# A projection's products in another order, splits woven into slabs, and a product with a scaled identity in place of scale and transpose

## The chip, the core and the metric

The kernel runs on one core of one Trainium2 chip, as one program. Its time is the device time of one execution in microseconds (us). The engines of the core run their own instruction streams side by side and wait for each other by semaphores: PE (TensorE) multiplies and transposes, DVE (VectorE), ACT (ScalarE) and POOL (GpSimd) work on tiles, and SP only issues DMAs here. PE reads its operands from SBUF and writes into the eight banks of PSUM. A PE transpose is one matmul instruction with the identity.

## The reference, cut to what matters

A first network (two layers of a hybrid mixer with a feed-forward part) makes `x`, 256 tokens of 1024 numbers. A second network of two layers follows, and the change is in that one alone. Of its layer:

```python
def modulate(x, shift, scale): return x * (1 + scale) + shift
for l in range(2):
    # context tokens (256): layer 0 whole, layer 1 only their k and v; latent tokens (256): whole
    h  = modulate(rms_norm_2(x, norm1_g[l]), sh1, sc1)
    p  = h @ w_in[l]                      # 1024 -> 2560: a (512), q (512), k (512), v (512), c (512)
    q, k = qk_heads(q, q_norm_g, rope), qk_heads(k, k_norm_g, rope)
    o  = diff_attn(q, k_all, v_all, lam)
    x += g1 * (concat[chunk_gmlp(a), rms_norm_2(o, subln_g), conformer_conv(c)] @ w_out)
    h2 = modulate(rms_norm_2(x, norm2_g[l]), sh2, sc2)
    x += g2 * ((silu(dwconv(h2 @ w_gate)) * (h2 @ w_val)) @ w_down)
def rms_norm_2(x, g): return x * rsqrt(mean(x * x) + EPS) * g
```

`conformer_conv` is a depthwise convolution of 31 taps over `a * sigmoid(g)` of the two halves of c, a layer norm and a silu. All is float32.

## The kernel before

Every product is made of high and low halves. A weight arrives in slabs of 256 rows by 512 columns (`SLAB_K` = 2 blocks of 128 rows). ACT rounds a slab into `whi`, DVE takes the rest into `wlo`, and the activations are kept the same way (`act2_h`, `act2_l`; the profile prints `act_h`, `act_l`). Each 128x128 block of an activation meets a slab's row block in three matmuls: high by high, high by low, low by high. Rows are tokens in tiles of 128: T = 4 tiles in layer 0 (latent and context), 2 in layer 1, except k and v and the first normalization there, which have 4. A slab of a 4-tile product is 24 matmuls of 512 columns, of a 2-tile product 12.

`Planner` (`plan_second`) lists `Step`s in one order. Each engine walks that same list and issues its own part of each step, so the list fixes the order on every engine. `weave(slabs, others)` puts a step `(at, st)` ahead of slab number `at`. At a slab's step ACT rounds and DVE splits the slab three ahead (`AHEAD`), which needs the buffer of the slab that PE used four before.

The steps that matter:

- `norm2`: POOL makes the root of each row (`rstd4`, L951, L926, L927), DVE multiplies `x` by it into `p` (L1387), one instruction a tile. `modsplit` k (eight, one for each 128 columns): PE turns that block of all tiles into one of banks 4 to 7 (L1776), DVE applies gain and shift (L1395), ACT makes the high half (L1100), DVE the low half (L1403, one step late). The first slab of the next product needs k = 0 and 1.
- the projection in five products of four slabs: c, q, k, a, v. Beside them: `cglu`, `cT` (PE turns c, ACT copies it to `cin`), `c_taps` in eight parts (DVE does the 31 taps of one half of the channels, L1525 and L1527; ACT weighs and POOL adds those of the other, L1160, L967, L974), `qk_sums` and `qk_scale` (DVE, L1420 to L1456; roots on POOL), `qkT2` (PE turns normalized q and k through banks 4 to 7, twice each; ACT copies the even ones out, DVE the odd ones, L1462), `gelu`, `ln`, `ln_scale` (L1542 to L1555).
- `agate` (PE, the product with `w_s`), which waits for `ln_scale` and stands first in the attention's list; then attention with units `att2_s`, `_v`, `_t`, `_e`, `_m`, and `subln` on its output.
- `ysplit` (eight: PE turns the merged branches, L1776, ACT and DVE L1408 make the halves), and `residual` with `w_out_2`.
- `norm2` again and the feed-forward part: per 512 columns `w_gate_2` and `w_val_2`, four PSUM banks each, in a turn over seven banks (`pl.turns = tuple(range(7))`); then `w_down_2` on banks 0 to 3.

## Time and profile before

| | |
|---|---|
| Median of three runs | 2446.95 us (2436.7 to 2447.53) |
| Profiled execution | 2444.05 us, its span 2442.4 us |
| PE busy in the span | 2222.0 us, 91% |
| DVE, ACT, POOL busy | 58%, 44%, 12% |
| The second network | from about 1356 us on |
| Idle PE ahead of transposes of `p`, whole span | 73.0 us |

The page shows busy times by engine and the costliest groups of instructions. What one place costs is read in the stretches of time, where each instruction has its start, its length and, in brackets, the idle time ahead of it with what ended it. A busy PE means that matmuls overlap: their starts, not their lengths, show the pace.

### The profile page before, as it was taken

The page shows a single profiled execution, that of the slowest core. Times are in us where ns is not written, and L with a number is a line of the kernel's source. Part 1 is how long each engine was busy: PE and PEld are TensorE (multiplying, and loading weights), DVE is VectorE, ACT ScalarE, POOL GpSimd, SP SyncE. Part 2 cuts the span into 40 slices and gives each one's busy share as a digit, 9 for nine tenths or more (in the row PEclk, how much of TensorE's full clock was granted, in tenths as well). Part 3 has the DMA queues.
Part 4 walks back from the last instruction along what each step waited for, and adds up shares of the span by engine and source line. Part 5 has one row for each costly group of instructions (what it writes and reads, how often), then busy time and mean ns, then how long its engine had stood idle before and what let it go on. Part 6 is the DMA issues. An engine that isn't in the chain of part 4 may idle for free. (4 is left out here: it accounts for less than half of the span.)

```text
span 2442.4 us, 31205 instructions
## 1 busy us (share of the span) xinstructions
PE 2222.0 (91%) x11948; PEld 1803.7 (74%) x11948; DVE 1421.3 (58%) x2234; ACT 1063.3 (44%) x1753; POOL 304.7 (12%) x310
## 2 busy tenths in 40 slices
PE   8998999899999989899999797789999998778999
PEld 6776677778777766777787675567888886658987
DVE  4655485554456555755454598755555337866664
ACT  4444555444344434554444454523232225454342
POOL 0007121100000062221000073100000001500000
PEclk9998999999999989999999898789999999889999
DMA  7553334466556534345656321222333334234654
GB/s 234 185 179 133 117 129 142 157 214 203 199 188 210 167 118 142 97 144 175 236 170 192 130 69 52 70 69 70 104 129 97 124 99 147 69 105 131 202 174 149
DMA packets 171842, 349.28 MB, mean 143 GB/s; under 512 B 11824, under 2 KB 23216, under 8 KB 171696
## 3 DMA queue, kind: packets, MB, share of 16 engines
q1 hardware_dynamic: 171696, 347.29, 43.7%
q8 instruction: 97, 1.59, 0.3%
q14 instruction: 49, 0.40, 0.1%
HBM read 346.19 MB, written 1.05 MB: 142 GB/s over the span
## 5 line engine op out<-in xcount | busy, mean ns | idle before, releaser
L820 DVE TENSOR_TENSOR wlo<-wraw,whi 128x1024 fp32r<-128x1024 f32 (+1 forms) x538 | 646.0, 1214 | 712.9 <-ACT whi L1017 710.9
L1017 ACT ACTIVATE whi<-wraw 128x1024 fp32r<-128x1024 f32 (+1 forms) x552 | 557.7, 1026 | 603.7 <-PE psum L1773 280.0
L1773 PE MATMUL psum<-whi,act_h 128*128 128x512 f32 (+2 forms) x1424 | 578.7, 406 | 30.4 <-DVE wlo L820 21.8
L1773 PE MATMUL psum<-wlo,act_h 128*128 128x512 f32 (+2 forms) x1424 | 557.4, 391 | 0.0
L1773 PE MATMUL psum<-whi,act_l 128*128 128x512 f32 (+2 forms) x1424 | 557.1, 391 | 0.0
L1773 PEld LDWEIGHTS psum<-whi,act_h 128*128 128x128 f32 x1424 | 275.6, 194 | 100.2 <-DVE wlo L820 25.6
L1773 PEld LDWEIGHTS psum<-whi,act_l 128*128 128x128 f32 x1424 | 274.4, 193 | 57.7
L1773 PEld LDWEIGHTS psum<-wlo,act_h 128*128 128x128 f32 x1424 | 275.4, 193 | 48.7
L1773 PE MATMUL psum<-act_h,whi 128*128 128x512 f32 (+1 forms) x704 | 243.8, 346 | 14.8 <-DVE cacc L1395 6.3
L1773 PE MATMUL psum<-act_l,whi 128*128 128x512 f32 (+1 forms) x704 | 239.6, 340 | 0.0
L1773 PE MATMUL psum<-act_h,wlo 128*128 128x512 f32 (+1 forms) x704 | 239.1, 340 | 0.0
L1773 PE MATMUL psum<-whi,hid_h 128*128 128x512 f32 x440 | 173.9, 395 | 0.8 <-DVE ft L1357 0.8
L1773 PE MATMUL psum<-wlo,hid_h 128*128 128x512 f32 x440 | 172.6, 392 | 0.0
L1773 PE MATMUL psum<-whi,hid_l 128*128 128x512 f32 x440 | 172.3, 392 | 0.0
L1773 PEld LDWEIGHTS psum<-act_h,whi 128*128 128x128 f32 x704 | 136.2, 193 | 32.9 <-issue 9.3
L1773 PEld LDWEIGHTS psum<-act_h,wlo 128*128 128x128 f32 x704 | 136.1, 193 | 14.4
L1773 PEld LDWEIGHTS psum<-act_l,whi 128*128 128x128 f32 x704 | 136.3, 194 | 13.2
L1776 PE MATMUL psum<-ident,p 128*128 128x128 f32 x228 | 44.4, 372 | 73.0 <-DVE p L1387 32.7
L1773 PEld LDWEIGHTS psum<-whi,hid_h 128*128 128x128 f32 x440 | 83.4, 190 | 19.2 <-DVE ft L1357 1.2
L1776 PEld LDWEIGHTS psum<-ident,p 128*128 128x128 f32 x228 | 40.0, 200 | 77.8 <-DVE p L1387 34.4
L1773 PEld LDWEIGHTS psum<-whi,hid_l 128*128 128x128 f32 x440 | 83.4, 190 | 17.7
L1773 PEld LDWEIGHTS psum<-wlo,hid_h 128*128 128x128 f32 x440 | 83.4, 189 | 17.1
(268 smaller groups left out, 2772.8 us busy)
## 6 DMA issues: line engine op xcount, KB each, us to landing
wraw<-in_w_in SPq DMA_DIRECT2D x136, 512.0 KB, 4.4
wraw<-in_w_gate SPq DMA_DIRECT2D x104, 512.0 KB, 4.2
wraw<-in_w_mod_pieces SPq DMA_DIRECT2D x96, 512.0 KB, 4.7
wraw<-in_w_ffn_in SPq DMA_DIRECT2D x80, 512.0 KB, 4.4
wraw<-in_w_ffn_out SPq DMA_DIRECT2D x44, 512.0 KB, 4.1
wraw<-in_w_down SPq DMA_DIRECT2D x44, 512.0 KB, 4.3
wraw<-in_w_val SPq DMA_DIRECT2D x40, 512.0 KB, 4.2
wraw<-in_w_branch SPq DMA_DIRECT2D x32, 512.0 KB, 4.8
```

The lines of the kernel that those rows point to most:

```text
L820: eng.tensor_tensor(wlo[:, i, 0:st.n, 0:st.w], wraw[:, st.s % RING_W, 0:st.n, 0:st.w], whi[:, i, 0:st.n, 0:st.w].bitcast(F32), ALU.subtrac ...
L1017: nc.scalar.activation(whi[:, d % RING_S, 0:st.n, 0:st.w], wraw[:, s % RING_W, 0:st.n, 0:st.w], ACT.Copy).then_inc(sem("slab_rounded"), 1)
L1773: return nc.tensor.matmul(out, lhsT, rhs, start=start, stop=stop)
L1776: return nc.tensor.transpose(out, src, ident[:, :])
```

## The change

Five things are altered, all in the second network.

1. `norm2`: DVE writes `diag`, the identity times the root of each row, 128x128 a tile, instead of `x` times the root. `modsplit` on PE multiplies `x` (stationary) with `diag` (moving) instead of transposing `p`; both are float32.
2. The eight `modsplit` steps stand no longer ahead of the product: four ahead of its first slab, two ahead of the second, two ahead of the third. The `ysplit` steps are woven into `w_out_2` likewise, whose slabs now go by row blocks 0, 6, 2, 4 (`order`).
3. The projection goes q, k, c, a, v. `qk_sums` and `qk_scale` come from slab 4 and slab 9 on, `cglu` at 13, `cT` at 14, the eight parts of the taps at 14 to 19, `qkT2` at 16 instead of 18, `gelu` at 18, `ln` at 19.
4. In attention, `subln` and its parts come behind the other steps of their round, not in the middle.
5. The turn of banks starts at bank 0 in the feed-forward part (`pl.gemm_banks = 0`).

```diff
+def gemm(..., order=None, **more):
+    order = order or range(0, nk, SLAB_K)
-        for k in range(0, nk, SLAB_K):
+        for at, k in enumerate(order):
...
+        def between(ss):
+            return [(0, st) for st in ss[:4]] + [(1, st) for st in ss[4:6]] + [(2, st) for st in ss[6:]]
...
-        gc = project(C_C, T, ready)
-        gq = project(C_Q, T)
+        gq = project(C_Q, T, ready)
         gk = project(C_K, 4)
+        gc = project(C_C, T)
...
-        for i, (g, tiles, at) in enumerate(((gq, T, 8), (gk, 4, 13))):
+        for i, (g, tiles, at) in enumerate(((gq, T, 4), (gk, 4, 9))):
...
-        others = [(5, cglu), (6, ct)] + [(at, st) for at, st in zip((7, 7, 11, 12, 12, 17, 17, 18), parts)]
-        others += qk + [(17, gelu), (18, qkt), (18, aln[0]), (19, aln[1])]
+        others = ss + [(13, cglu), (14, ct)] + [(at, st) for at, st in zip((14, 15, 15, 16, 17, 17, 18, 19), parts)]
+        others += qk + [(18, gelu), (16, qkt), (19, aln[0]), (20, aln[1])]
-        pl.steps += weave(gc + gq + gk + ga + gv, others)
+        pl.steps += weave(gq + gk + gc + ga + gv, others)
...
-                    att += pending[:1]
+                    behind += pending[:1]
...
+            att += behind
...
-        residual("w_out_2", "act2", KD, 0, {st.k: drained(st.bank) for st in ss}, True)
+        residual("w_out_2", "act2", KD, 0, {st.k: drained(st.bank) for st in ss}, True, between(ss), order[::SLAB_K])
-        pl.turns = tuple(range(7))
+        pl.turns, pl.gemm_banks = tuple(range(7)), 0
...
-                        dve.tensor_scalar(p[:, t, 0:D], x[:, t, :], rstd4[:, t:t + 1], None, ALU.mult
+                        dve.tensor_scalar(diag[:, t, :], ident[:, :], rstd4[:, t:t + 1], None, ALU.mult
...
-                        ins = turn(psum[:, st.bank[0], t * P:(t + 1) * P], p[:, t, a:a + P])
+                        ins = dot(psum[:, st.bank[0], t * P:(t + 1) * P], x[:, t, st.k * P:(st.k + 1) * P], diag[:, t, :])
```

On DVE in layer 0 of the second network, before, the copies of turned q and k (L1462) stand behind the last taps, and the layer norm follows:

```order
L1436 TENSOR_TENSOR p<-p,ssq 128x512
L1439 TENSOR_TENSOR p<-p,rows 128x512
L1527 SCALAR_TENSOR_TENSOR cacc<-cin,cols,cacc 128x2x243
L1527 SCALAR_TENSOR_TENSOR cacc<-cin,cols,cacc 128x2x242
L1527 SCALAR_TENSOR_TENSOR cacc<-cin,cols,cacc 128x2x241
L1462 COPY qT<-psum 128x512 x2
L1462 COPY kT<-psum 128x512 x2
L1542 TENSOR_REDUCE lnm<-p 128x4
```

At the same place on DVE of the changed kernel (its line numbers are 5 higher here), the copies are L1467 and the taps L1530 and L1532:

```order
L1532 SCALAR_TENSOR_TENSOR cacc<-cin,cols,cacc 128x2x253
L1532 SCALAR_TENSOR_TENSOR cacc<-cin,cols,cacc 128x2x254
L1532 SCALAR_TENSOR_TENSOR cacc<-cin,cols,cacc 128x2x255
L1467 COPY qT<-psum 128x512 x2
L1467 COPY kT<-psum 128x512 x2
L825 TENSOR_TENSOR wlo<-wraw,whi 128x1024
L1532 SCALAR_TENSOR_TENSOR cacc<-cin,cols,cacc 128x2x255
L1532 SCALAR_TENSOR_TENSOR cacc<-cin,cols,cacc 128x2x254
```

The copies moved ahead of the last 15 taps, but they stand behind the first 16, all of which now come behind the last `qk_scale`.

PE turns q and k in that step; with the semaphores that it waits for, in the changed kernel (the row of three more that follows each of these is left out):

```order
L1781 MATMUL psum<-ident,p 128x128 [waits psum_free5,qk_normed]
...
L1781 MATMUL psum<-ident,p 128x128 [waits psum_free6]
...
L1781 MATMUL psum<-ident,p 128x128 [waits psum_free7]
...
L1781 MATMUL psum<-ident,p 128x128 [waits psum_free4]
...
L1781 MATMUL psum<-ident,p 128x128 [waits psum_free5]
...
L1781 MATMUL psum<-ident,p 128x128 [waits psum_free6]
...
L1778 MATMUL psum<-whi,act_h 128x512 [waits psum_free0,slab_split]
```

The fifth and sixth of the eight groups take banks 5 and 6 again, which ACT's and DVE's first copies free; four slabs of v stand behind this step (two before).

On PE at the start of layer 0's feed-forward part, before, the last transposes and the first matmuls of `w_gate_2` are:

```order
L1776 MATMUL psum<-ident,p 128x128 [waits psum_free7,xn_out]
L1776 MATMUL psum<-ident,p 128x128 x3
L1776 MATMUL psum<-ident,p 128x128 [waits psum_free4,xn_out]
L1776 MATMUL psum<-ident,p 128x128 x3
L1773 MATMUL psum<-act_h,whi 128x512 [waits slab_split,psum_free4,mod_lo]
```

In the changed kernel the first slab's matmuls wait for other banks, and the products with `diag` stand between slabs:

```order
L1778 MATMUL psum<-act_h,whi 128x512 [waits slab_split,psum_free0,mod_lo]
...
L1778 MATMUL psum<-act_h,whi 128x512 [waits psum_free3]
...
L1778 MATMUL psum<-act_h,wlo 128x512
L1778 MATMUL psum<-diag,x 128x128 [waits psum_free5,xn_out]
L1778 MATMUL psum<-diag,x 128x128 x3
L1778 MATMUL psum<-diag,x 128x128 [waits psum_free6,xn_out]
L1778 MATMUL psum<-diag,x 128x128 x3
```

The first slab takes banks 0 to 3 instead of 4, 5, 6 and 0, and half of the turning moved behind it.

## Rows read from the trace of the kernel before

**Rows 1.** The costliest groups: transposes of `p`, busy and mean, idle before and releasers
```profile
L1776 PE MATMUL psum<-ident,p 128*128 128x128 f32 x228 | 44.4, 372 | 73.0 <-DVE p L1387 32.7
```

**Rows 2.** Stretches: length; busy (count) of PE, PEld, DVE, ACT, POOL; PEclk; DMA
```profile
1475.00:1491.00 16.00, 0.00 (x0) 0.00 (x0) 15.58 (x15) 4.72 (x5) 9.04 (x6) 0.56 0.22 66
...
1653.00:2000.00 347.00, 346.68 (x1633) 284.13 (x1634) 161.83 (x195) 98.04 (x128) 0.00 (x0) 0.99 0.33 105
```

**Rows 3.** In order of time (start, length), layer 0: normalization, slab pace, a small operation
```profile
1356.09 2.74 DVE L1387 TENSOR_SCALAR p<-x,rstd 128x1024 f32<-128x1024 f32 x4 [3.72 <-POOL rstd L927]
...
1358.89 5.96 PE L1776 MATMUL psum<-ident,p 128*128 128x128 f32 x28 [11.44 <-DVE p L1387]
...
1363.67 0.68 DVE L1403 TENSOR_TENSOR act_l<-cacc,act_h 128x512 fp32r<-128x512 f32 x1
...
1366.01 0.47 PE L1773 MATMUL psum<-whi,act_h 128*128 128x512 f32 x1
...
1378.37 1.23 DVE L820 TENSOR_TENSOR wlo<-wraw,whi 128x1024 fp32r<-128x1024 f32 x1 [1.88 <-ACT whi L1017]
1383.81 1.23 DVE L820 TENSOR_TENSOR wlo<-wraw,whi 128x1024 fp32r<-128x1024 f32 x1 [4.21 <-ACT whi L1017]
...
1523.30 0.35 DVE L1483 TENSOR_SCALAR p<-psum,ri 128x128 f32<-128x128 f32 x1
```

**Rows 4.** In order of time, layer 0: taps, turning of q and k, `ln`, gate
```profile
1403.93 9.92 DVE L1527 SCALAR_TENSOR_TENSOR cacc<-cin,cols,cacc 128x482 f32<-128x482 f32 x7
...
1433.88 13.82 POOL L974 TENSOR_TENSOR cacc<-cacc,ctmp 128x504 f32<-128x504 f32 x8 [2.33 <-ACT ctmp L1160]
...
1446.51 7.32 DVE L1527 SCALAR_TENSOR_TENSOR cacc<-cin,cols,cacc 128x504 f32<-128x504 f32 x8
...
1474.10 2.25 DVE L820 TENSOR_TENSOR wlo<-wraw,whi 128x1024 fp32r<-128x1024 f32 x1
1491.06 5.20 PE L1776 MATMUL psum<-ident,p 128*128 128x128 f32 x32 [16.47 <-DVE p L1439]
1493.07 0.69 DVE L1462 COPY qT<-psum 128x512 f32<-128x512 f32 x1
...
1496.90 1.21 DVE L1542 TENSOR_REDUCE lnm<-p 128x4 f32<-128x1024 f32 x1
...
1504.52 1.22 DVE L1555 TENSOR_TENSOR p<-p,rows 128x1024 f32<-128x1024 f32 x1
1507.01 1.89 PE L1773 MATMUL psum<-p,wsT 128*128 128x256 f32 x8
```

**Rows 5.** PE in order of time: transposes; float32 products at full and half clock
```profile
1398.79 1.03 PE L1776 MATMUL psum<-ident,p 128*128 128x128 f32 x8
...
1534.26 1.13 PE L1773 MATMUL psum<-p,aT 128*128 128x128 f32 x8
...
2175.89 2.08 PE L1773 MATMUL psum<-p,aT 128*128 128x128 f32 x8
```

**Rows 6.** PE in order of time, layer 0: merged branches, and start of the feed-forward part
```profile
1583.67 3.65 PE L1776 MATMUL psum<-ident,p 128*128 128x128 f32 x16 [3.34 <-DVE act_l L1408]
...
1639.67 5.62 PE L1776 MATMUL psum<-ident,p 128*128 128x128 f32 x28 [7.62 <-DVE p L1387]
...
1653.33 0.77 PE L1773 MATMUL psum<-act_h,whi 128*128 128x512 f32 x1 [6.30 <-DVE cacc L1395]
```

**Rows 7.** Layer 1: normalization, taps, turning of q and k, gate, start of `w_down_2`
```profile
2033.01 4.70 PE L1776 MATMUL psum<-ident,p 128*128 128x128 f32 x24 [7.63 <-DVE p L1387]
...
2061.82 5.32 DVE L1527 SCALAR_TENSOR_TENSOR cacc<-cin,cols,cacc 128x241 f32<-128x241 f32 x7
...
2120.96 5.09 PE L1776 MATMUL psum<-ident,p 128*128 128x128 f32 x24 [11.58 <-DVE p L1439]
...
2137.66 0.71 PE L1773 MATMUL psum<-p,wsT 128*128 128x128 f32 x4 [0.24 <-ACT p L1063]
...
2377.62 0.51 PE L1773 MATMUL psum<-whi,hid_h 128*128 128x512 f32 x1 [0.77 <-DVE ft L1357]
```

More of the change, by code:

```diff
@@ L161, in weave, with gemm @@
     return out + slabs[i:]
-def gemm(pl, weight, layer, act, tiles, nk, col0, width, evac, row0=0, kt0=0, ready=(), turned=False, **more):
+def gemm(pl, weight, layer, act, tiles, nk, col0, width, evac, row0=0, kt0=0, ready=(), turned=False, order=None, **more):
     steps = []
+    order = order or range(0, nk, SLAB_K)
     hasdict = isinstance(ready, dict)
@@ L171, in gemm @@
             banks.append(pl.gemm_bank())
-        for k in range(0, nk, SLAB_K):
+        for at, k in enumerate(order):
             n = min(SLAB_K, nk - k)
-            last = k + n == nk
+            last = at == len(order) - 1
             st = Step(kind="slab", s=len(pl.slabs), weight=weight, layer=layer, row=row0 + k, n=n, col=col0 + a, w=w,
-                      act=act, kt=kt0 + k, tiles=tiles, banks=banks, first=k == 0, last=last, c=c, a=a, evac=evac,
+                      act=act, kt=kt0 + k, tiles=tiles, banks=banks, first=at == 0, last=last, c=c, a=a, evac=evac,
                       turned=turned, **more)
@@ L197, in gemm @@
             elif (pl.mod_queue or pl.mod_last) and tiles == 2 and st.s >= 3 * RING_W:
-                at, slabs_in = k // SLAB_K, -(-nk // SLAB_K)
-                if pl.mod_queue and at % 4 == 0 and at + 3 < slabs_in:
+                if pl.mod_queue and at % 4 == 0 and at + 3 < len(order):
                     st.after = mod_ride(pl, pl.next_bank())
@@ L439, in norm @@
                        halves=[("mod_half", pl.tick("mod_half"))] if tiles == 4 else []) for k in range(KD)]
-            pl.steps += ss
-            return {st.k: [("mod_lo", st.lo)] for st in ss}
-        ready = norm(0, 4, l > 0)
+            return {st.k: [("mod_lo", st.lo)] for st in ss}, between(ss)
+        def between(ss):
+            return [(0, st) for st in ss[:4]] + [(1, st) for st in ss[4:6]] + [(2, st) for st in ss[6:]]
+        ready, ss = norm(0, 4, l > 0)
         pl.first_slab[l] = len(pl.slabs)
@@ L760, in build @@
         rstd4 = sb("rstd4", [P, 4], F32, two)
+        diag = sb("diag", [P, 4, P], F32, two)
         kT = sb("kT", [P, B_HEADS, 4 * P], F32, two)
@@ L1843, in _ @@
                     ins.then_inc(full(bk), 1)
-                if st.kind in ("modsplit", "ysplit"):
+                if st.kind == "modsplit":
                     need(pe, st.waits)
                     fill(pe, st.bank)
-                    a = st.k * P if st.kind == "modsplit" else st.col
                     for t in range(st.tiles):
-                        ins = turn(psum[:, st.bank[0], t * P:(t + 1) * P], p[:, t, a:a + P])
+                        ins = dot(psum[:, st.bank[0], t * P:(t + 1) * P], x[:, t, st.k * P:(st.k + 1) * P], diag[:, t, :])
+                    ins.then_inc(full(st.bank), 1)
+                if st.kind == "ysplit":
+                    need(pe, st.waits)
+                    fill(pe, st.bank)
+                    for t in range(st.tiles):
+                        ins = turn(psum[:, st.bank[0], t * P:(t + 1) * P], p[:, t, st.col:st.col + P])
                     ins.then_inc(full(st.bank), 1)
```

18 lines of the change are left out of this document (9 added, 9 removed).

## The prediction

> **What bounds the kernel now.** I read the busy shares and costliest groups first. PE is the bound, but its transposes of `p` have 73.0 us of idle time ahead of them [rows 1]: PE stands there waiting for somebody's vector work. The stretches say where. In the feed-forward part of layer 0 PE is busy 346.68 of 347 us, while from 1475 to 1491 us it is busy for nothing and DVE for 15.58 [rows 2]. The order of time then gives four kinds of hole: the scaling of `x` ahead of a normalization's first transpose [rows 3, 6, 7], the wait for the last `qk_scale`, 16.47 us in layer 0 and 11.58 in layer 1 [rows 4, 7], 3.34 us ahead of the last merged branches, and 6.30 us ahead of the first matmul of `w_gate_2` in layer 0 [rows 6]. The change aims at each. The question at each is what is late next. Below, S is the start of PE's first transpose after a normalization before the change, S' the same place after it.
>
> **Prices.** A slab of 24 matmuls takes PE 5.44 us (two DVE splits that each follow a freed slab, 1378.37 and 1383.81) [rows 3], of 12 matmuls 2.72. A transpose takes 0.11 us at full clock (8 in 1.03, the last one's tail of some 0.2 taken off) [rows 5] and 0.21 at half clock (28 in 5.96) [rows 3]. The product with `diag` isn't in the trace. Its nearest row is the float32 product `psum<-p,aT`, also of 128 by 128. It has two records for each instruction: four instructions a unit give x8. That is 0.125 us a record at full clock and 0.24 at half [rows 5], so 0.25 and 0.48 us an instruction. The bounds are one record (the transposes' price) and the 0.48. I take two records.
>
> The Trainium skill (TensorE: Matmul & The Clock Gate, "Terms") says that transpose mode is 4 times faster for FP32. The trace shows a factor of 2.3 at full clock. By the page's factor the woven products of a 4-tile stage would take 7 us, not 4, and the sum would be some 9 us worse.
>
> **Normalization.** DVE writes 128 columns a tile instead of 1024. Four of the old take 2.74 us; a 128-column operation with a scalar takes 0.35 at most [rows 3], and overlapped somewhat less. I take 0.15 us each between ends of 0.1 and 0.35. S' is therefore S - 2.1 us with four tiles (ends 2.3 and 1.3) and S - 1.0 with two.
>
> Then, layer 0, first normalization. Before, the first slab starts at S + 7.1 (1366.01 - 1358.89), and `act_l` of k = 1 was ready at S + 5.5 (1363.67 + 0.68) [rows 3]. After, 16 instructions stand ahead: 32 records, the first 20 at half clock, 6.3 us; with DVE's first block 1 us later, the first slab starts at about S' + 6.8. The other 16 instructions cost 2 us behind each of two slabs. Four slabs end at S' + 6.8 + 21.8 + 4 = S' + 32.6 = S + 30.5, against S + 28.9: 1.6 us later. The woven splits of the slabs (each 1.23 us [rows 3] in DVE's chain and a rounding that it waits for, some 2.2 us) stay behind PE here. In layer 1 the q slabs have only 2.72 us and DVE's chain is the bound: k = 7 is ready at about S' + 21, the four slabs end at S' + 23.7.
>
> **Projection, layer 0.** `cT` now follows slab 13. It ends at S' + 32.6 + 10 x 5.44 + 1 = S' + 88, and the taps start at S' + 89.5. All 31 stand behind this point, and so do DVE's three last slab splits and four copies, and POOL's 31. Taps beside POOL's go at 1.42 us (7 in 9.92), alone at 0.92 (8 in 7.32), a split beside POOL at 2.25 [rows 4]. POOL pairs with DVE there; I take 1.48 a tap for it, between 1.42 and the 1.73 of another stretch (8 in 13.82) [rows 4], so some 46 us, to S' + 135.5. In its time DVE does three splits (6.7), four copies (1 us each between 0.69 and 1.4) and 24 taps; 7 more at 0.92 end at S' + 142. `ln` to `ln_scale` took 8.8 us, from 1496.90 to 1505.74 [rows 4]. So `ln_out` comes at S' + 150.5 = S + 148.4. Before, the gate's product started at 1507.01 = S + 148.1. The 16.47 us are gone, and given back: +0.3 us.
>
> PE meanwhile: `qkT2` starts at S' + 99. Its sixth group needs DVE's first copy, which stands behind 16 taps, at S' + 117. PE idles about 16 us in the middle of `qkT2`, then does four slabs of v, 22 us and 2 for a half clock, to S' + 143, still ahead of `ln_out`.
>
> **Projection, layer 1.** After S' + 23.7: k 21.8, c 10.9, half of a 5.4: S' + 61.8. `cT` waits until DVE has made `cglu` behind three `qk_scale` of k, at 65.7. Taps from 68.3 at 0.76 each (7 in 5.32) [rows 7]; 16 of them and two splits of some 1.6 (between 1.23 and 2.25) bring the copies at 83.7. PE leaves `qkT2` at 86, and four slabs of v (21.8, 2 for the half clock) end at S' + 109.8 = S + 107.7. `ln_out` is ready at S' + 104.5. Before, the gate started at 2137.66 = S + 104.65 [rows 7]. So +3.0 us. The cover of before, only two slabs behind `qkT2`, is gone.
>
> **Merged branches.** The first slab may start with DVE's second low half, at 1584.2, not at 1587.0 after 16 transposes [rows 6]. But PE has been idle then, and runs at half clock for some 5.5 us; before, transposes took that time, now a slab does, at 0.43 us a matmul. 14 slow ones cost 2.8 us. +0.4 in layer 0, 0 in layer 1.
>
> PE's clock by the rows: 28 transposes alone brought it from half to full in about 5.7 us, since 28 took 5.96 and the matmuls after 1366.01 ran full [rows 3]. The Trainium skill (TensorE: Matmul & The Clock Gate, "Part 4: PE-mode transpose") says that transposes don't raise the clock. This trace contradicts it. By the page, real products would warm PE up earlier than before and each stage would gain about 2 us more.
>
> **Feed-forward part.** Layer 0: before, PE waits for bank 4, which holds the turned block k = 7 until DVE has read it, so the first slab starts at S + 13.7 (1653.33 - 1639.67), cold [rows 6], and four end at S + 13.7 + 21.8 + 2.3 = S + 37.8. After, with banks 0 to 3 free, S + 30.5 as above: -7.3 us, the one clear gain. PE is full behind it [rows 2], so it stays. Layer 1 has two tiles, no such wait, and the woven float32 products: +0.9. But the last product's banks are now 0 and 1, and so are the first of `w_down_2`; before only the second bank waited, 0.77 us [rows 7], behind 1.4 us of other matmuls: +1.4.
>
> **Attention.** Moving `subln` back lets DVE make `e` up to 1.3 us earlier in some rounds and later in the next; cold PE after a long stall costs about as much. 0, between -3 and +3.
>
> **Sum.** 0.3 + 0.4 - 7.3 + 3.0 + 0 + 0.9 + 1.4 + 0 = -1.3 us. On the profiled execution's 2444.05 that is 2442.8; it lies 2.9 under the median, within the spread of the three runs. I predict 2443. What a measurement of this kernel can tell from no change is about 0.5%, 12 us.
>
> **Rivals.**
> - *The stall really goes.* If DVE's taps aren't slowed by POOL, they go at 0.92 throughout. The copies come 12 us sooner, `ln_out` at S' + 133.5, the gate in layer 0 17 us earlier and in layer 1 5 us earlier than in the forecast: 2443 - 22 = 2421. For it: POOL now runs in one block, and the short q and k operations no longer beside it. Against: a tap beside POOL's took 1.42 in the plainest stretch [rows 4].
> - *The taps become the bound* (slower). If both engines keep POOL's 1.73 us a tap in layer 0 [rows 4] and 0.93 in layer 1 (0.76 in the same proportion), `ln_out` in layer 0 comes at S' + 158 (+7), the copies in layer 1 3 us later, and attention, with PE at half clock after 30 idle us, costs its full 3: 2443 + 13 = 2456. It decides from a tap pace of about 1.7 us on.
> - *`diag` costs a transpose.* With one record an instruction, each 4-tile stage gains some 3 us and the 2-tile one 1: 2443 - 10 = 2433. Against: every float32 product in the trace has two records.
> - *`diag` costs four transposes*, 0.44 us an instruction at full clock: each 4-tile stage loses 3 us more than in the forecast: 2443 + 9 = 2452. Against: the 0.125 a record [rows 5]. This is what the page's factor would give.
> - *PE warms up sooner* by real products than by transposes: four stages gain 2 us, 2443 - 8 = 2435. Against: transposes alone brought the full clock [rows 3]. This is the page's rule on transposes.
>
> **Chances.** Forecast 0.58, own range 2434 to 2452. Stall goes 0.17, taps bound 0.14, cheap `diag` 0.05, dear `diag` 0.03, warm PE 0.03. Faster by over 0.5% (under 2435) is the first rival and a share of the third: 0.20. Slower by over 0.5% (above 2459) is half of the second and the errors of the forecast that point there: 0.13. Within: 0.67. The range takes in the nearer half of the first rival and most of the second: 2424 to 2457.
>
> **What would show it.** In the changed trace: two records for each `diag` product of about 0.125 us; the idle time ahead of `p` transposes in `qkT2` not 16.47 but split, with 10 us or more ahead of its fifth or sixth group, released by ACT's or DVE's copies; the gate's product released by `ln_scale`, 15 us or more after v's last slab in layer 0 and at once in layer 1; no wait of 6 us ahead of `w_gate_2`; 0.8 to 2 us ahead of layer 1's `w_down_2`. A gate in layer 0 earlier than S' + 145 would make the projection's step wrong, and a feed-forward gain under 5 us the one gain.

## The result, and the profile after

The changed kernel takes 2444.36 us (median of 20 runs), the kernel before 2438.82 us in 20 runs beside them: ratio 1.0024, 95% interval 1.0013 to 1.0035. It is slower by about 6 us, a quarter of a per cent. A later set of 12 runs gave 1.0007, interval 0.9991 to 1.0023, which taken alone shows no loss. The prediction was 2443 us, as a gain of 1.3; the sign was wrong. That 2444.36 lies so near to 2443 is luck: the forecast stood on a profile of 2444.05 and a median of three of 2446.95, and 20 runs put the kernel before at 2438.82.

The profiled execution took 2446.99 us (span 2445.4; before 2442.4). PE's idle time ahead of its turning work, 73.0 us [rows 1], is now 26.2 ahead of the products with `diag` and 25.8 ahead of the other transposes. Part of it has only moved: waits for `act_l` between slabs and ahead of the gate, shown below, are new. The first fence is the costliest groups, the second the order of time of PE in layer 0's first normalization.

```profile
L1778 PE MATMUL psum<-diag,x 128*128 128x128 f32 x224 | 35.3, 326 | 26.2 <-DVE diag L1392 26.2
...
L1781 PE MATMUL psum<-ident,p 128*128 128x128 f32 x116 | 19.2, 321 | 25.8 <-ACT qT L1125 16.3 <-DVE qT L1467 5.8 <-DVE p L1523 3.7
```
```profile
1360.87 5.43 PE L1778 MATMUL psum<-diag,x 128*128 128x128 f32 x32 [9.57 <-DVE diag L1392]
...
1368.06 0.47 PE L1778 MATMUL psum<-whi,act_h 128*128 128x512 f32 x1 [1.76 <-DVE act_l L1408]
...
1373.62 1.95 PE L1778 MATMUL psum<-diag,x 128*128 128x128 f32 x16
1376.46 0.47 PE L1778 MATMUL psum<-whi,act_h 128*128 128x512 f32 x1 [0.90 <-DVE act_l L1408]
```
```profile
1359.94 0.88 DVE L1392 TENSOR_SCALAR diag<-ident,rstd 128x128 f32<-128x128 f32 x4 [3.71 <-POOL rstd L932]
```

DVE makes `diag` in 0.88 us where the scaled `x` took 2.74 [rows 3], so PE starts 1.9 us earlier, counted from its last matmul ahead of the wait. But the first slab starts 7.2 us behind PE's start (1368.06 - 1360.87), for 7.1 before, and the next two slabs each stand behind a woven block: 1.95 us of products and 0.90 of waiting for `act_l`. Before, four slabs ran without a break. The same pattern stands in all four normalizations; in the two-tile one, layer 1's second, the waits ahead of the woven slabs are 0.63 us. DVE's part of one woven block (start, length):

```profile
1370.80 1.22 DVE L825 TENSOR_TENSOR wlo<-wraw,whi 128x1024 fp32r<-128x1024 f32 x1 [1.11 <-ACT whi L1022]
1374.77 0.99 DVE L1400 TENSOR_SCALAR cacc<-psum,modg,modT 128x256 f32<-128x256 f32 x2 [2.74 <-PE psum L1778]
1375.68 0.68 DVE L1408 TENSOR_TENSOR act_l<-cacc,act_h 128x512 fp32r<-128x512 f32 x1
```

DVE is idle for 2.74 us, and its reading of the turned block starts at 1374.77, only when PE, in order behind a whole slab, has reached the block; the slab then waits for the `act_l` that starts at 1375.68.

The turning of q and k and the gate in layer 0, PE first, then DVE and POOL, answering to [rows 4]:

```profile
1450.28 1.03 PE L1781 MATMUL psum<-ident,p 128*128 128x128 f32 x8
...
1462.05 1.91 PE L1781 MATMUL psum<-ident,p 128*128 128x128 f32 x16
...
1473.49 1.11 PE L1781 MATMUL psum<-ident,p 128*128 128x128 f32 x4 [9.53 <-ACT qT L1125]
1479.34 2.82 PE L1781 MATMUL psum<-ident,p 128*128 128x128 f32 x12 [4.74 <-DVE qT L1467]
...
1517.71 3.72 PE L1778 MATMUL psum<-p,wsT 128*128 128x256 f32 x8 [12.97 <-DVE p L1560]
```
```profile
1452.67 3.89 DVE L1532 SCALAR_TENSOR_TENSOR cacc<-cin,cols,cacc 128x482 f32<-128x482 f32 x3
1456.48 2.26 DVE L825 TENSOR_TENSOR wlo<-wraw,whi 128x1024 fp32r<-128x1024 f32 x1
1458.66 12.42 DVE L1532 SCALAR_TENSOR_TENSOR cacc<-cin,cols,cacc 128x488 f32<-128x488 f32 x8
1471.01 2.27 DVE L825 TENSOR_TENSOR wlo<-wraw,whi 128x1024 fp32r<-128x1024 f32 x1
1473.20 5.49 DVE L1532 SCALAR_TENSOR_TENSOR cacc<-cin,cols,cacc 128x504 f32<-128x504 f32 x4
...
1484.07 13.49 DVE L1532 SCALAR_TENSOR_TENSOR cacc<-cin,cols,cacc 128x510 f32<-128x510 f32 x8
1498.04 10.85 DVE L1532 SCALAR_TENSOR_TENSOR cacc<-cin,cols,cacc 128x494 f32<-128x494 f32 x7 [0.49 <-DVE cacc L1532]
```
```profile
1453.28 24.07 POOL L979 TENSOR_TENSOR cacc<-cacc,ctmp 128x482 f32<-128x482 f32 x15
1483.67 24.71 POOL L979 TENSOR_TENSOR cacc<-cacc,ctmp 128x510 f32<-128x510 f32 x15 [6.31 <-ACT ctmp L1165]
```

The wait of 16.47 us is now 9.53 and 4.74 inside `qkT2`, and 12.97 ahead of the gate. DVE's 30 taps are five rows of 3.89, 12.42, 5.49, 13.49 and 10.85 us: 46.1 us, 1.54 each. Beside them run POOL's 30 additions, 1.6 us each with one pause of 6.31 us, and they end with DVE's taps (at 1508.4 and 1508.9). Before, the same 30 took 9.92 + 6.39 + 7.32 + 7.98 + 2.24 = 33.9 us.

In the feed-forward part of layer 0 the 6.30 us wait [rows 6] has gone, and the woven blocks have come; in layer 1 the last wait, ahead of `w_down_2`, has grown from 0.77 [rows 7] to 2.48 us:

```profile
1645.88 6.24 PE L1778 MATMUL psum<-diag,x 128*128 128x128 f32 x32 [5.75 <-DVE diag L1392]
...
1653.19 0.47 PE L1778 MATMUL psum<-act_h,whi 128*128 128x512 f32 x1 [1.06 <-DVE act_l L1408]
...
1658.75 1.95 PE L1778 MATMUL psum<-diag,x 128*128 128x128 f32 x16
1661.60 0.47 PE L1778 MATMUL psum<-act_h,whi 128*128 128x512 f32 x1 [0.90 <-DVE act_l L1408]
...
2379.25 0.47 PE L1778 MATMUL psum<-whi,hid_h 128*128 128x512 f32 x1 [2.48 <-DVE ft L1362]
```

**Why one pair of profiles can't carry this.** Both kernels run the same instructions up to PE's last matmul of the first network. That point, called E here, comes at 1347.06 us before and 1350.92 after, and in the twelve other profiles of this study between 1333.6 and 1355.9. One place where the pair parts (the stretch; its length; busy time and count of PE, PEld, DVE, ACT, POOL; PEclk; DMA), before and then after:

```profile
487.00:492.00 5.00, 5.00 (x23) 4.10 (x23) 2.40 (x3) 2.70 (x4) 0.00 (x0) 1.00 0.81 259
```
```profile
487.00:492.00 5.00, 5.00 (x23) 3.83 (x15) 2.36 (x2) 2.74 (x5) 0.00 (x0) 0.66 0.72 226
```

The same matmuls follow waits of 1.40 and 1.95 us; the one run stays at full clock, in the other a stretch runs at 0.66 and loses 1.5 us. A like wait doesn't settle it either: in the changed kernel's two profiles PE waits 2.48 us ahead of layer 1's `w_down_2`, and the granted clock in the 5 us behind that wait is 1.00 in the one and 0.71 in the other. So stages are compared below from E on, with two profiles of each of the two kernels.

| stage, us | before | changed |
|---|---|---|
| E to the gate, layer 0 | 159.95, 160.14 | 166.79, 166.93 |
| gate to first `ysplit` (attention) | 70.39, 70.36 | 68.48, 69.96 |
| `ysplit` to last of `w_out_2` | 54.26, 52.78 | 53.56, 53.51 |
| to first of `w_down_2` | 273.88, 273.06 | 270.02, 270.01 |
| `w_down_2` | 119.45, 119.46 | 119.55, 119.56 |
| to the gate, layer 1 | 111.82, 111.37 | 114.35, 114.36 |
| attention | 45.44, 45.51 | 42.49, 42.50 |
| `ysplit` to last of `w_out_2` | 31.14, 30.90 | 31.04, 31.04 |
| to first of `w_down_2` | 161.83, 161.66 | 162.05, 161.24 |
| `w_down_2` | 60.79, 60.78 | 59.70, 61.13 |
| E to PE's last matmul | 1088.95, 1086.02 | 1088.03, 1090.24 |

On the means the second network is 1.6 us longer, with single stages between -3.5 and +6.8. Repeats of one kernel differ by up to 1.5 us in a stage, so a difference of 1 us in one pair of stages tells nothing.

### The profile page after: what moved, and what is told of

Its sections match the earlier page's. It is cut to its first block and busy times, and to the rows that moved or that the text cites. A ratio compares the mean times of both kernels' runs of the same rounds, so it can differ in the third digit from the quotient of the medians.

```text
span 2445.4 us, 31429 instructions
## 1 busy us (share of the span) xinstructions
PE 2228.5 (91%) x12060; PEld 1811.2 (74%) x12060; DVE 1411.7 (58%) x2234; ACT 1063.3 (43%) x1753; POOL 303.6 (12%) x310
## 5 line engine op out<-in xcount | busy, mean ns | idle before, releaser
L1778 PE MATMUL psum<-whi,y_h 128*128 128x512 f32 x192 | 80.6, 420 | 0.1
L1778 PE MATMUL psum<-whi,y_l 128*128 128x512 f32 x192 | 77.2, 402 | 0.0
```

Of the source, the lines that this page charges most:

```text
L1778: return nc.tensor.matmul(out, lhsT, rhs, start=start, stop=stop)
```

## The experiments

Ratios are to the kernel before, run on the same chip; the last column is E to PE's last matmul in the profile, for which before has 1087.5 (mean of two).

| run | median us | ratio, 95% interval | second network |
|---|---|---|---|
| e1 old order | 2442.47 | 1.0005 (0.9990 to 1.0020) | 1088.60 |
| e2 subln, banks | 2433.32 | 0.9971 (0.9957 to 0.9985) | 1078.24 |
| e3 no diag | 2451.76 | 1.0051 (1.0035 to 1.0066) | 1095.25 |
| e4 changed again | 2438.94 | 1.0007 (0.9991 to 1.0023) | 1090.24 |
| e5 splits ahead | 2431.89 | 0.9968 (0.9950 to 0.9985) | 1079.61 |
| e6 diag beside e2 | 2427.32 | 0.9952 (0.9935 to 0.9969) | 1074.49 |
| e7 order beside e2 | 2432.31 | 0.9975 (0.9962 to 0.9989) | 1082.65 |
| e9 before again | 2440.64 | 1.0005 (0.9986 to 1.0023) | 1086.02 |
| e8 light additions | 2415.06 | 0.9892 (0.9875 to 0.9909) | 1060.72 |
| e10 all good parts | 2425.82 | 0.9935 (0.9917 to 0.9953) | 1070.24 |
| e11 e6 again | 2427.88 | 0.9937 (0.9919 to 0.9955) | 1072.67 |
| e12 copies first | 2426.90 | 0.9939 (0.9924 to 0.9953) | 1074.72 |

### e1: the old order in the changed kernel

```
- gq, gk, gc, ga, gv; cglu 13, cT 14, taps 14, 15, 15, 16, 17, 17, 18, 19; qk 4, 9; qkT2 16
+ gc, gq, gk, ga, gv; cglu 5, cT 6, taps 7, 7, 11, 12, 12, 17, 17, 18; qk 8, 13; qkT2 18
```


> The changed kernel with the projection's order of before: c, q, k, a, v, the taps, qk steps and qkT2 behind the same slabs as before. diag, woven splits, subln behind and banks from 0 stay. E is PE's last matmul of the first network. In the profiles gate's product in layer 0 came at E + 159.95 before and at E + 166.79 after; in layer 1 at 111.8 and 114.4 us behind the last w_down matmul of layer 0. Theory (the taps): DVE's 30 taps took 33.9 us before and 46.1 after, since POOL's 31 now stand beside them from the first to the last; the splits and diag cost the projection nothing. Then the old order brings the gate to E + 160 to 162 (the 16 us wait ahead of qkT2 is back) and layer 1's to 111 to 113, and the time is 6 to 9 us under the changed kernel's, 2436 to 2438. Rival (weaving and diag cost it): PE's woven float32 products and the 0.9 us waits for act_l delay every later piece, the gate stays at E + 165 or later, and the time within 3 us of the changed kernel's.

The gate in layer 0 came at E + 164.91: at the rival's 165, not at 160 to 162. Layer 1's came at 115.20, 0.8 later than with the new order, not sooner. So the order is 2 us of the 6.8, and my theory of the taps explains the smaller part. What is left of the change costs the projection 4 to 5 us. The second network, 1088.60 us, is as long as the changed kernel's 1089.1, and the time missed the theory's 2436 to 2438.

### e2: subln behind and the banks alone

```
  behind = []; ... behind += pending[:1]; behind.append(subs[-1]); ... att += behind
- pl.turns = tuple(range(7))
+ pl.turns, pl.gemm_banks = tuple(range(7)), 0
```


> The kernel before with two parts of the change alone: subln and its root and scale behind a round's e and m, and the feed-forward part's banks from 0. Theory: each is a gain of its own. Attention (gate to first ysplit) goes from 70.4 to about 68.5 us in layer 0 and from 44.6 to about 41.6 in layer 1; the first w_gate slab comes 6 us sooner behind PE's first transpose (13.7 to about 7.5), and the stretch from w_out's last matmul to w_down's first from 270.0 to 264. Sum 9 to 11 us: 2428 to 2430. Rival: the attention gain came from the projection's order (v's slabs end long before the gate), so that attention stays at 70 and 44.5, and only 6 us are gained: 2433.

Attention took 67.76 and 42.54 us: subln's place is worth 2.6 and 2.9 by itself, which I had priced at 0. `w_out_2` to `w_down_2` in layer 0 took 265.75, a gain of 7.7 where the whole change gains 3.5: four of the banks' eight microseconds are lost again by another part. In layer 1 the same stretch grew by 2.7, to 164.49. The gate in layer 0 came at E + 161.34 though nothing ahead of it was changed (before: 159.95 and 160.14): that is how far equal work can lie apart. The time, 2433.32, is the rival's 2433 and not the theory's 2428 to 2430, though the attention gain went the theory's way; layer 1's 2.7 is most of the rest. PE in layer 0 now waits only for DVE's reads, 1.10 at most, and the first slab starts 7.1 us behind the start:

```profile
1639.93 4.39 PE L1778 MATMUL psum<-ident,p 128*128 128x128 f32 x24 [7.62 <-DVE p L1389]
...
1646.65 0.63 PE L1778 MATMUL psum<-ident,p 128*128 128x128 f32 x4 [1.10 <-DVE cacc L1397]
```

### e3: scaled x and transposes in the changed kernel

```
- dve.tensor_scalar(diag[:, t, :], ident[:, :], rstd4[:, t:t + 1], None, ALU.mult
+ dve.tensor_scalar(p[:, t, 0:D], x[:, t, :], rstd4[:, t:t + 1], None, ALU.mult
- dot(psum, x, diag)
+ turn(psum, p)
```


> The changed kernel with DVE's scaling of x to p and transposes of p, as before, in place of diag and its float32 products; the weaving and all else stay. Theory (diag costs more than it saves): DVE's scaling makes PE's start 1.9 us later in 4-tile stages and 0.9 in the 2-tile one, but 16 transposes at half clock take 3.4 us for 5.4, and each 16 woven take 1.8 for 2.0 (0.11 us for 0.125 a record, 16 for 32 records from 2 x 8): 8 woven transposes 0.9 for 1.95. A 4-tile stage then is 0 to 2 us shorter, the time 0 to 5 us under the changed kernel's. Rival (diag is the gain it looks): the woven products are hidden behind DVE's splits, which PE waits 0.9 us for either way, so that only DVE's 1.9 us count: each stage 2 us longer, the time 5 to 7 us over the changed kernel's.

Slower than the changed kernel, 1.0051, as the rival had it and by more. The woven transposes show why they save nothing:

```profile
1355.40 3.67 PE L1781 MATMUL psum<-ident,p 128*128 128x128 f32 x16 [11.44 <-DVE p L1392]
1360.96 0.77 PE L1778 MATMUL psum<-whi,act_h 128*128 128x512 f32 x1 [1.89 <-DVE act_l L1408]
...
1367.84 1.04 PE L1781 MATMUL psum<-ident,p 128*128 128x128 f32 x8
1370.23 0.47 PE L1778 MATMUL psum<-whi,act_h 128*128 128x512 f32 x1 [1.35 <-DVE act_l L1408]
```

The first slab starts 1.6 us sooner behind PE's start (5.56), but it is cold, at half clock for part of its time, and takes 6.9 us for 5.6. A block of transposes takes 1.04 us for 1.95, and the wait behind it grows from 0.90 to 1.35: 2.4 against 2.85 a block, 0.9 a stage, less than the 1.9 that DVE gives up. The larger difference is in the feed-forward part of layer 1, 165.99 us for 161.65 (e11 takes it up).

### e4: the changed kernel again

> The changed kernel once more, for a second profile. The profiled pair differs by 3.0 us, of which 3.9 lie in the first network, where both do the same; the 20 timed pairs differ by 5.6. Theory: the clock after a stall steps up at chance moments, 1 us or so a stall, and the first profile of the changed kernel had a lucky second network; the second network's length here is 1090 to 1096 us for 1088.0, and single stages differ by up to 1 us. Rival: stages repeat to 0.3 us and the first network is what the change slowed: E comes again 3 to 5 us later than in before's profile.

Second network 1090.24, at the lower edge of the theory's 1090 to 1096, which isn't clear of the first profile's 1088.03; E at 1341.31, 10 us sooner than the first time. The two gates and `w_down_2` of layer 0 repeat to 0.15 us; attention in layer 0 and `w_down_2` in layer 1 differ by 1.5 and 1.4, more than the theory's 1. The rival, that the change slows the first network, is out.

### e5: all modsplit blocks ahead in the changed kernel

```
- return {...}, between(ss)
+ return {...}, [(0, st) for st in ss]
```


> The changed kernel with all eight modsplit blocks ahead of the first slab, as before the change; diag, its products, the new order and all else stay. In the changed kernel's profile each 4-tile stage has two woven blocks between its first slabs, 2.85 us apiece (1.95 of products, 0.90 of waiting for act_l), and the first slab starts no earlier than with everything ahead (7.2 us behind PE's start, for 7.1). Theory (the weaving is a loss): ahead, the first slab starts some 10 us behind PE's start instead of 7.2, no slab waits after that, and four slabs end at 32 for 34.7: each 4-tile stage gains 2.8, the 2-tile one 1, and the second network takes 1079 to 1082 us for the 1088.0 and 1090.2 of the changed kernel's two profiles; 2433 to 2437. Rival (the weave is worth its wait): 64 records ahead take 11 us or more, each slab still finds its act_l late, and the stages stay within 1 us.

As the theory said, and by somewhat more. Against the changed kernel the gate in layer 0 comes 3.8 us sooner (163.11), the feed-forward stretch is 3.6 shorter (266.40), layer 1's gate 3.0 sooner (111.31), its feed-forward 0.9 shorter: 11.3 us, of which the second network as a whole shows 9.5 (1079.61 for 1089.1); the time goes from 1.0007 or 1.0024 to 0.9968. The `ysplit` steps stay woven here; their stage takes 53.6 us woven and 52.8 to 54.3 in the kernel before, so their weave shows no gain and no loss. All 64 records stand in one row, and the first slab follows 9.5 us behind the start without waiting, nor does a slab after it:

```profile
1343.56 9.73 PE L1778 MATMUL psum<-diag,x 128*128 128x128 f32 x64 [9.57 <-DVE diag L1392]
1353.05 0.48 PE L1778 MATMUL psum<-whi,act_h 128*128 128x512 f32 x1
```

### e6: diag beside e2's two parts, old order, all ahead

```
+ diag = sb("diag", [P, 4, P], F32, two); DVE writes diag; modsplit: dot(psum, x, diag)
```


> The kernel before with subln behind and the feed-forward part's banks from 0 (2433.32 us in its own run), and beside them diag and its products in place of the scaled x and the transposes; all eight blocks ahead, old order. Theory: DVE saves 1.9 us at a 4-tile stage, PE's 64 records take about 10 us where 32 transposes and DVE's splits took 7.1, so the first slab is 1 us later than without diag: three stages +1, the 2-tile one 0: 2434 to 2438. Rival (diag is free or a gain): the products keep ahead of DVE's splits, the first slab stays 7.1 behind PE's start, which itself is 1.9 earlier: 2426 to 2429.

2427.32, within the rival's 2426 to 2429. But the mechanism is neither. The first slab came 9.3 us behind PE's start, for e2's 7.1 in the feed-forward part, and the three 4-tile stages stayed within 0.6 of e2's (gates 161.50 and 111.46, feed-forward 266.30): DVE's 1.9 us and PE's 2.2 cancel. The gain is in layer 1's feed-forward part, 160.47 for 164.49.

### e7: the new order beside e2's two parts

```
  e1's edit the other way round, on e2
```


> The kernel before with subln behind and banks from 0 (2433.32 us in its own run), and beside them the projection's new order and placing; scaled x and transposes, all ahead. Theory: the order alone costs layer 0 some 2 us and gains layer 1 under 1, since the 46 us of taps beside POOL's take what the wait ahead of qkT2 gives: gate at E + 162 to 164 in layer 0 (E: PE's last matmul of the first network; before 159.95, with the two parts 161.34), time 2433 to 2436. Rival (the order is the gain once the weaving is off): with four slabs done by S + 28.9, taps, copies and ln all come 4 us sooner than in the changed kernel and PE's v slabs cover them: gate at E + 156 or earlier, 2428 or less.

Gate at E + 162.61, 1.3 later than in e2, layer 1's 0.5 later, attention in layer 0 1.2 longer (68.98). With e5 and e1 that gives the order a cost of 1 to 2 us at the gate and 1 to 2 in the attention behind it, where PE starts at half clock after its idle time (the gate's eight products took 3.78 us here, for 1.89 before [rows 4]). Each of these is near to what repeats differ by; three pairs agree on the gate's sign (1.3 here, 2.0 in e1, 1.6 to 2.5 between e5 and e6 or e11). The rival's gain isn't there.

### e8: POOL's additions on 8 columns

```
+ o, part = o[:, :, 0:8], part[:, :, 0:8]
  pool.tensor_tensor(o, o, part, ALU.add)
```


> The changed kernel, with POOL's 30 additions of weighted taps done on the first 8 of each sequence's columns alone (the rest of its half of the convolution isn't computed), so that POOL hardly runs beside DVE's taps; DVE's own taps are whole. Theory (DVE and POOL slow each other): DVE's taps in layer 0 take 0.75 to 0.92 us each, not 1.54, all 30 some 25 us and not 46; the copies for qkT2 come some 10 us sooner, PE's wait inside qkT2 falls from 14 us to under 5, and the gate is left to PE's v slabs, at S' + 132 to 138 instead of S' + 156.8: the first stage 20 us shorter, layer 1's 3 to 5, time 2416 to 2422. Rival (the taps are slow by themselves in this place, by ACT's work or their shapes): they stay at 1.3 us or more and the gate moves by less than 8 us.

The kernel leaves out most of POOL's half of the convolution. DVE's taps in layer 0, the same instructions as in the fence after the change:

```profile
1450.40 2.56 DVE L1532 SCALAR_TENSOR_TENSOR cacc<-cin,cols,cacc 128x482 f32<-128x482 f32 x3
1452.87 1.24 DVE L825 TENSOR_TENSOR wlo<-wraw,whi 128x1024 fp32r<-128x1024 f32 x1
1454.04 6.24 DVE L1532 SCALAR_TENSOR_TENSOR cacc<-cin,cols,cacc 128x488 f32<-128x488 f32 x8
...
1461.33 3.09 DVE L1532 SCALAR_TENSOR_TENSOR cacc<-cin,cols,cacc 128x504 f32<-128x504 f32 x4
...
1469.81 6.32 DVE L1532 SCALAR_TENSOR_TENSOR cacc<-cin,cols,cacc 128x510 f32<-128x510 f32 x8
1476.61 5.41 DVE L1532 SCALAR_TENSOR_TENSOR cacc<-cin,cols,cacc 128x494 f32<-128x494 f32 x7 [0.49 <-DVE cacc L1532]
```
```profile
1463.73 0.66 PE L1781 MATMUL psum<-ident,p 128*128 128x128 f32 x4 [2.01 <-ACT qT L1125]
1465.08 2.82 PE L1781 MATMUL psum<-ident,p 128*128 128x128 f32 x12 [0.69 <-DVE qT L1467]
1490.84 1.99 PE L1778 MATMUL psum<-p,wsT 128*128 128x256 f32 x8 [1.13 <-DVE p L1560]
```

2.56 + 6.24 + 3.09 + 6.32 + 5.41 = 23.6 us for 46.1: 0.78 a tap. A slab split between them takes 1.24 for 2.26. The waits in `qkT2` are 2.01 and 0.69, the gate comes at S' + 132.2, 24.7 us sooner than after the change. That DVE and POOL slow each other is shown, and so is its price here. POOL's 30 instructions are all still there: on 16 columns (8 of each of two sequences) they take 0.2 us at the shortest and mostly 0.7, as long as the tap beside them. In layer 1 the gate is 4.3 sooner. (Two engines that share 60 taps need 46 us; DVE alone, at 0.78, would need 47. All taps on DVE wasn't tried, and no run has POOL's whole additions without DVE beside them.)

### e9: the kernel before again

> The kernel before once more, for a second profile. Its one profile has a second network of 1088.95 us, and the changed kernel's two have 1088.0 and 1090.2, though it is some 4 us slower over all timed runs. Theory: before's one profile had an unlucky second network (clock steps), and the usual one is 1083 to 1087 us. Rival: it is 1089 again, and the 4 us lie in the first network, whose end was at 1347.06 before and at 1350.92 and 1341.31 after the change.

The second network took 1086.02, within the theory's 1083 to 1087, though E came at 1355.93, the latest of all. The first profile had been 2.9 longer, 1.5 of it in `w_out_2` and 0.8 in the feed-forward part of layer 0.

### e10: the good parts together

```
  e6, and: ss: [(0, six blocks), (1, the last two)] woven into the first slabs
+ pl.gemm_banks += 2 * l        # ahead of w_down_2
```


> The kernel before with subln behind, banks from 0 and diag (2427.32 us in its own run as diag alone), old order, and two things more: six modsplit blocks ahead and the last two behind the first slab, a slab ahead of their use; and w_down_2 of layer 1 beginning on banks 2 and 3. Theory (in the change's weave each block stood directly ahead of the slab that reads it, so PE waited for DVE's split of it): now no slab waits for act_l. The first slab starts 8 to 8.7 us behind PE's start (9.5 with eight ahead, 7.2 with four), one woven block costs 1.95, and four slabs end at 31.5 to 32.3, where eight ahead give 31.3 and the change's weave 34.7: as good as all ahead within 1 us. The wait of 2.48 us ahead of w_down_2 in layer 1 goes or is under 1. Time 2424 to 2428. Rival (a product between slabs costs more than its records, weave or wait): the stage is again 3 us longer than with eight ahead and the time 2434.

No slab waits for `act_l`; the woven block costs its 1.95 us and nothing more:

```profile
1358.71 7.26 PE L1776 MATMUL psum<-diag,x 128*128 128x128 f32 x48 [9.56 <-DVE diag L1390]
...
1371.48 1.95 PE L1776 MATMUL psum<-diag,x 128*128 128x128 f32 x16
```

The stages are those of e6 and e11 (gate 161.35, feed-forward 266.38): a weave a slab ahead of its use is no loss and no gain. No wait stands ahead of `w_down_2` in layer 1; `w_out_2` to the end of the program's matmuls takes 217.49 us there, for 221.78 in e6 and 219.04 in e11. 2425.82 us, 0.9935: the best of the complete kernels, by less than the interval against e11 and e12.

### e11: e6 again

> The kernel before with subln behind, banks from 0 and diag, once more, for comparison with the run beside it on one chip and for a second profile: 2427 us, stages within 0.5 us of its first profile. Of interest is w_out's last matmul of layer 1 to the first w_down matmul, 160.47 us with diag and 164.49 without: theory, the longer waits for DVE's ft without diag let the clock fall, 0.91 in a stretch of 20 us behind a wait of 2.19 us, and with diag the same wait is 0.49 and the clock stays 1.00, so it is 160 to 162 again. Rival: chance, and it is 164 this time.

159.30 us, so the feed-forward gain of layer 1 repeats: 159.1 to 160.7 in the profiles of e5, e6, e11 and e12, with `diag` and all ahead, 161.2 to 162.4 with `diag` and the weave (after, e4, e1, e8), and 164.3 to 166.0 in those of e2, e3 and e7, without `diag`. (The kernel before has 161.8 without it, but on the old banks.) The stretch that holds the first wait for `ft` shows the clock (columns as above), e2 and then e6:

```profile
2248.70:2268.70 20.00, 17.81 (x146) 17.27 (x146) 11.95 (x18) 6.91 (x10) 0.00 (x0) 0.91 0.50 167
```
```profile
2248.70:2268.70 20.00, 18.31 (x161) 17.57 (x159) 13.29 (x20) 7.85 (x11) 0.00 (x0) 1.00 0.66 233
```

In e2 PE waited 2.19 us for `ft` and then ran part of the stretch at half clock, in e6 it waited 0.49 and stayed at full. All profiles sort this way: the wait is 1.7 to 2.2 us in the five without `diag` and at most 0.8 in the nine with it. The longer wait is 1.7 us of the 4.0 between e2 and e6, and a granted clock of 0.91 over 20 us is worth another 1.8. PE stands at the same place at the same time in both runs when the wait begins (2254.4 and 2254.5). Why DVE is later with `ft` in the one than in the other isn't settled.

The start of this stage shows a second difference, e2 and then e6, PE's first turning instruction at 2208.7 in both:

```profile
2213.90:2216.50 2.60, 2.60 (x14) 2.60 (x14) 2.19 (x6) 1.01 (x3) 0.00 (x0) 0.50 0.00 0
```
```profile
2213.90:2216.50 2.60, 2.60 (x25) 2.60 (x24) 2.33 (x6) 0.86 (x3) 0.00 (x0) 1.00 0.00 0
```

With `diag` the full clock is back 5.1 to 5.6 us behind PE's start in all nine profiles, with transposes 7.8 to 8.2 in all five. In e6 PE had been busy without a break since its start, in e2 with idle times of 0.24 and 0.35 us between transposes; whether the breaks or the kind of instruction makes the difference wasn't tried apart. It makes up for the first slab, which starts 1.6 us later with `diag`.

### e12: the copies ahead of the taps

```
- (16, qkt)
+ (14.5, qkt)      # on e5: qkT2 behind slab 15, ahead of all but the first four taps
```


> The changed kernel with all modsplit blocks ahead (2431.89 us), and qkT2 put one slab sooner, ahead of all but the first four taps, so that DVE's and ACT's copies stand ahead of the rest. Theory (the taps are the bound of the new order, not the copies): PE's wait inside qkT2 falls from some 14 us to under 4, but the gate is released by the same ln_scale behind the taps and comes at E + 160 to 163, for 163.1; gain 0 to 3, 2429 to 2432. Rival (the copies' place is what costs): PE's v slabs and POOL's pause of 6 us were on the path too, and the gate comes at E + 157 or sooner, 2426.

```profile
1445.95 2.35 PE L1781 MATMUL psum<-ident,p 128*128 128x128 f32 x20
1448.71 1.53 PE L1781 MATMUL psum<-ident,p 128*128 128x128 f32 x12 [0.42 <-DVE qT L1467]
...
1461.15 0.77 PE L1778 MATMUL psum<-whi,act_h 128*128 128x512 f32 x1 [5.42 <-ACT p L1068]
...
1505.59 3.78 PE L1778 MATMUL psum<-p,wsT 128*128 128x256 f32 x8 [19.74 <-DVE p L1560]
```

`qkT2` no longer waits (0.42), and the idle time has moved behind it: 5.42 us ahead of v's last four slabs, where PE waits for ACT, and 19.74 ahead of the gate, which comes at E + 161.60, 1.5 sooner than in e5. So in layer 0 the taps, not the copies, bound the new order. In layer 1 the gate came 2.4 sooner (108.94), the earliest of any, but the attention behind it took 44.40 us for 42.50. The time, 2426.90, is nearer to the rival's 2426 than to the theory's 2429 to 2432, and not by the rival's mechanism: of the 4.9 us by which the second network is shorter than e5's, 3.2 lie in layer 1's feed-forward part and `w_down_2`, which the edit doesn't touch.

## Why the prediction was wrong

By its own terms, measured on the means of two profiles each:

| term | forecast | measured |
|---|---|---|
| layer 0 normalization to gate | +0.3 | +6.8 |
| attention and merged branches, layer 0 | +0.4 | -1.1 |
| layer 0 feed-forward | -7.3 | -3.5 |
| layer 1 normalization to gate | +3.0 | +2.8 |
| attention and merged branches, layer 1 | 0 | -3.0 |
| layer 1 feed-forward and `w_down_2` | +2.3 | -0.5 |
| sum | -1.3 | +1.6 |

(`w_down_2` of layer 0, not forecast, is the 0.1 that is missing.)

The rows miss by +6.5, -1.5, +3.8, -0.2, -3.0 and -2.8 us. Most of that cancels, so a sum within 3 us is luck too. Two steps failed, one in an overlap and one in a price.

**The overlap that failed** is the one on the woven splits: "stay behind PE here". I priced a woven block at its 2 us of PE time and let DVE's chain (read, round, subtract) run behind the slab. It can't: PE issues in order, so DVE gets the block only after the slab ahead of it, and the slab that reads it is next. Two blocks cost 2.85 us each, the first slab starts only 2.3 us sooner than with all eight ahead (7.2 us behind PE's start for 9.5), and the weave loses 3.8, 3.6, 3.0 and 0.9 us (e5; on the old order, e1 against e6 and e11, 3.9, 3.6, 3.4 and 1.7). It is the largest single cost of the change. In layer 0 I had four slabs end at S' + 32.6; they ended at S' + 34.9 in the first normalization and at S' + 35.0 in the feed-forward part. There I put the whole weave inside a gain of 7.3, of which the banks alone bring 7.7 (e2); with all blocks ahead the gain is 7.1 (e5). My own bound, a gain under 5 there, says that term was wrong. In layer 1, where I did let DVE's chain bound the slabs, the term came out right.

**The taps** are the price that failed. The mechanism was named right and its size too small: 1.48 us a tap for 24 and 0.92 for 7, 42 us, where all 30 took 1.54, 46.1. The copies behind the first 16 came at S' + 117.7 for my 117; it is the last seven, which I let run alone for 6.4 us, that took 10.85. There was no stretch in which DVE ran alone, since ACT, which makes POOL's weighted taps, stood in `qkT2` behind PE's wait: POOL pauses for 6.31 us and so ends with DVE. The 0.92 was misread besides. Those eight taps of the kernel before (shortest, median and longest in ns) are one that began beside POOL's last addition and others without it:

```profile
L1527 DVE SCALAR_TENSOR_TENSOR cacc<-cin,cols,cacc x8: 744/748/1734, 1446.5 to 1453.1; 128x504 f32<-128x504 f32 x2, 128x506 f32<-128x506 f32 x2, 128x508 f32<-128x508 f32 x2, 128x510 f32<-128x510 f32 x2
```

Alone a tap takes 0.75 us, and the trace of before could have said so. The gate at S' + 156.8 for my 150.5 is 4.2 of this, 1.7 of the weave's waits (taps from S' + 91.2 for 89.5), and 0.4 in the `ln` behind them. It lies nearer to the rival "the taps become the bound" (S' + 158) than to the forecast, but with a pace of 1.54, not its 1.7. The rival "the stall really goes" failed on the contention: with POOL's additions cut short (e8) the gate comes at S' + 132.2, and the rival had `ln_out` at S' + 133.5. Of the signs I had named for layer 0, two came smaller: 9.53 and 4.74 us ahead of `qkT2`'s fifth and sixth group for "10 us or more" at one of them, and 12.97 ahead of the gate for 15.

**diag.** Right: two records an instruction, 1.95 us for 16 records, 0.122 a record, neither the cheap nor the dear `diag` of the rivals. The Trainium skill (TensorE: Matmul & The Clock Gate, "Terms") gives transposes of FP32 a factor of 4. Measured on the same blocks at full clock, 8 transposes in 1.04 us (e3) stand against 8 products in 1.95, a factor of 1.9, or 2.1 with the row's tail of 0.2 taken off both. What I missed is that all ahead it balances with DVE's gain (e6), and that it helps the feed-forward part of layer 1 by some 4 us, where the forecast had +0.9 for `diag` and the weave (e11). That is most of the row's -2.8.

**Attention.** "0, between -3 and +3" for subln's place was 2.6 and 2.9 us of gain (e2). I called the two effects equal without a row. The new order gives 1 to 2 of it back in layer 0.

**Banks of w_down_2 in layer 1.** +1.4 forecast; the wait went from 0.77 to 2.48 us, so 1.7, and went away with other banks (e10).

**PE's warming up.** The rival had the full clock come sooner behind products than behind transposes, for a gain of 8 us. In the first normalization the full clock was back 3.4 and 4.9 us behind PE's start with `diag` and 5.6 and 6.0 before (two profiles each); in the 4-tile stages of all runs, 2.9 to 6.2 and 2.9 to 8.5, neither kind is sooner throughout. In the 2-tile stage it does come some 3 us sooner (e11), which pays for the later first slab and no more. The rule of the Trainium skill (TensorE: Matmul & The Clock Gate, "Part 4: PE-mode transpose") that transposes don't bring the full clock, which stood behind the rival, isn't borne out: before the change PE did nothing but 28 transposes from 1358.89 on, and the granted clock was 0.50 up to 1364.4 and 1.00 behind it.

**Sum of the parts**, from the stages of e1 to e7 and e11: weave +11 to +13, order +3, diag -4 to -5, banks -7.7 in layer 0 and +3 in layer 1, subln -5.5. That is -1 to +2, and the profiles say +1.6. The 20 timed runs say 3.2 to 8.5 us and the later 12 -2.2 to 5.6. A remainder of some 2 us between profiles and times stays open; clock steps that differ by chance, as at 487 us above, are of that size, but that they make it up wasn't shown.

## What to carry to other kernels

A preparation woven between products must stand one product ahead of the one that reads it, or the in-order engine waits at each block for the end of the chain through the other engines (0.90 us here); and it is worth weaving only if the first product starts sooner by more than the blocks cost. When a wait is taken away by gathering another engine's work into one block, ask what runs beside that block: here DVE and POOL together did about as many taps in a microsecond (60 in 46 us) as DVE alone (30 in 23.6). Price a change of many parts part by part, and try the parts apart: three of the five were gains of 4 to 6 us each, and two threw them away.

## What the runs showed of the hardware

- DVE's float32 taps beside POOL's additions take 1.54 us (after), with those additions cut to 16 columns 0.78 (e8), and in the kernel before 0.75 where POOL is idle; a slab split takes 2.26 and 1.24. DVE's 30 taps take 22.5 us longer beside POOL's 30 additions than beside the short ones. That would fit two engines taking turns at one resource; no run shows which.
- The same instructions of the first network ended between 1333.6 and 1355.9 us in 14 profiles. The granted clock after a short wait differed from run to run (1.00 and 0.71 behind the same wait of 2.48 us), so a stage measured from a common mark tells some 1.5 us where the whole time doesn't tell 5.
- A wait of 2.19 us ahead of a matmul was followed by a stretch at 0.91, one of 0.49 by a stretch at 1.00: a wait can cost more than its length.
- In the 2-tile stage the full clock was back 5.1 to 5.6 us behind PE's start on float32 products in nine profiles, and 7.8 to 8.2 behind its start on transposes, with short breaks, in five.
